# Second block's attention: the older group's value sums follow the third chunk of a unit's transposes and no longer the second

## The reference

```python
def scores(qn_, qr_, kn_, kr_):
    s = jnp.einsum('bqhd,bkhd->bhqk', qn_, kn_) + jnp.einsum('bqhr,bkr->bhqk', qr_, kr_)
    return s.astype(jnp.float32) * scale

def attend(blk):
    qn_b, qr_b = blk
    s = jnp.concatenate([scores(qn_b, qr_b, kn, kr), scores(qn_b, qr_b, knc, krc)], axis=-1)
    p = jax.nn.softmax(s, axis=-1).astype(v.dtype)
    return (jnp.einsum('bhqk,bkhd->bqhd', p[..., :L], v)
            + jnp.einsum('bhqk,bkhd->bqhd', p[..., L:], vc))
```

## Time and profile before

| | us |
|---|---|
| median of 3 runs | 3123.01 (3120.47 to 3127.02) |
| the profiled execution | 3127.2 |
| its span | 3125.4 |
| TensorE busy in the span | 2817.5 (90%) |
| VectorE, ScalarE, GpSimd busy | 1834.8, 883.5, 668.6 |
| mean granted TensorE clock | 0.954 of 2.4 GHz |

### The profile page before, as it was taken

The page is one execution under the profiler, slowest core; times in us unless marked ns, Lnnn a source line. Parts: engine busy times, 40 slices in busy tenths (PEclk is TensorE's granted clock), DMA queues, the critical chain, the costliest instruction groups (busy, mean ns, idle before and its releaser), DMA issues. The chain is left out here.

```text
span 3125.4 us, 30778 instructions
## 1 busy us (share of the span) xinstructions
PE 2817.5 (90%) x11545; PEld 1900.7 (61%) x11545; DVE 1834.8 (59%) x2979; ACT 883.5 (28%) x1527; POOL 668.6 (21%) x408
## 2 busy tenths in 40 slices
PE   5999888988679979999998799996999998999968
PEld 1444444547545548667777699995778885444456
DVE  5644009999576657765841355553685533887553
ACT  1111013100323332245333555552332221111122
POOL 0000000004021112333421333323332220333222
PEclk9999999999879989999999899998999998999979
DMA  2113100000100023333745233223421113111042
GB/s 74 71 72 131 44 20 28 34 34 22 54 1 1 1 91 112 116 127 137 268 168 178 78 88 78 55 58 115 142 88 48 46 69 145 57 57 57 27 168 101
DMA packets 103896, 254.91 MB, mean 82 GB/s; under 512 B 17728, under 2 KB 33768, under 8 KB 99465
## 3 DMA queue, kind: packets, MB, share of 16 engines
q1 hardware_dynamic: 103754, 253.02, 24.3%
HBM read 195.20 MB, written 57.78 MB: 81 GB/s over the span
## 5 line engine op out<-in xcount | busy, mean ns | idle before, releaser
L310 PE MATMUL psum<-part,part 128*128 128x512 f32 (+1 forms) x1984 | 776.7, 391 | 74.9 <-DVE part L2564 25.5
L311 PE MATMUL psum<-part,part 128*128 128x512 f32 (+1 forms) x1984 | 739.3, 373 | 0.0
L312 PE MATMUL psum<-part,part 128*128 128x512 f32 (+1 forms) x1984 | 738.7, 372 | 0.0
L1529 POOL TENSOR_TENSOR part<-arena,part 128x1024 fp32r<-128x1024 f32 (+2 forms) x155 | 353.3, 2280 | 872.5 <-ACT part L1523 872.3
L310 PEld LDWEIGHTS psum<-part,part 128*128 128x128 f32 x1984 | 376.9, 190 | 161.9 <-POOL part L1529 58.1
L311 PEld LDWEIGHTS psum<-part,part 128*128 128x128 f32 x1984 | 377.5, 190 | 78.4 <-issue 12.2
L312 PEld LDWEIGHTS psum<-part,part 128*128 128x128 f32 x1984 | 376.4, 190 | 71.0
L218 PE MATMUL psum<-arena 128*128 128x512 f32 (+1 forms) x672 | 231.8, 505 | 14.7 <-DMA arena<-in_w_f 10.0
L1523 ACT ACTIVATE part<-arena 128x1024 fp32r<-128x1024 f32 (+2 forms) x155 | 149.6, 965 | 271.1 <-PE psum L312 202.4
L2270 DVE TENSOR_REDUCE arena<-psum 128x1 f32<-128x1280 f32 x64 | 95.4, 1491 | 206.4 <-PE psum L2221 206.4
L627 PE MATMUL psum<-arena 128*128 128x512 f32 x464 | 202.1, 597 | 5.7 <-DVEq L417 5.7
(11 more groups left out here) (306 smaller groups left out, 4025.3 us busy)
## 6 DMA issues: line engine op xcount, KB each, us to landing
arena<-in_ada_w SPq DMA_DIRECT2D x24, 1024.0 KB, 6.1
arena<-in_w_hy SPq DMA_DIRECT2D x40, 512.0 KB, 3.2
scratch_spec<-arena SPq DMA_DIRECT2D x68, 256.0 KB, 2.0
arena<-scratch_spec SPq DMA_DIRECT2D x12, 1024.0 KB, 5.3
arena<-in_w_out SPq DMA_DIRECT2D x16, 512.0 KB, 3.6
arena<-in_w_mgate SPq DMA_DIRECT2D x16, 512.0 KB, 4.2
arena<-in_w_mout SPq DMA_DIRECT2D x16, 512.0 KB, 3.7
arena<-in_w_hout SPq DMA_DIRECT2D x16, 512.0 KB, 3.5
```

Of the source, the lines that this page charges most:

```text
L310: nc.tensor.matmul(acc, a_hi, b_hi, start=start, stop=False)
L311: nc.tensor.matmul(acc, a_hi, b_lo, start=False, stop=False)
L312: return nc.tensor.matmul(acc, a_lo, b_hi, start=False, stop=stop)
L1529: self.K.nc.gpsimd.tensor_tensor(self.lo[s][:, 0:n], self.raw[s][:, 0:n], self.hi[s][:, 0:n].bitcast(F32), ALU.subtract).then_inc(self.spl ...
```

## The change

In TensorE's loop the call for the third chunk is put ahead of the values, so that all ten transposes of a unit stand together and the values follow them. The condition on u is tested a second time as a block of its own. Nothing else is changed: no wait, no buffer, no other engine's list.

```diff
@@ -2255,10 +2255,10 @@
                     pe.wait_ge(exped, u + 1)
                     turn(u, 0)
                     turn(u, 1)
+                if 0 <= u < NU:
+                    turn(u, 2)
                 if i >= 3 and (i - 3) // 2 < NU // 2:
                     add_values((i - 3) // 2, (i - 3) % 2)
-                if 0 <= u < NU:
-                    turn(u, 2)
```

## The result

The changed kernel's median is 3230.9 us (4 runs, 3225.66 to 3237.81) against 3123.0 before: a ratio of 1.0346, 95% interval 1.0321 to 1.037. The forecast was 3230.6. The profiled execution of the changed kernel has a span of 3236.0 us, 110.6 more than before.

The account below looks back on a forecast made before the run. TensorE was taken to bound the changed stage; 107.4 us for 60 intervals and 0.2 for the last stretch, added to 3123.0, gave 3230.6 us. Forecast's own range 3224 to 3236; 8-in-10 range 3219 to 3248.

Parts of the forecast that it names:

- The bound: In the changed stage TensorE is busy 362.37 of 367 us, so whatever is added to its path comes out at the end.
- the sum: Over the changed stage: 107.4 us for 60 iteration intervals plus 0.2 at the end, +107.6 us.
- the clock rival: TensorE's clock falls in the new gaps before chunk 2, slower still: 3248 us (one in six) to 3333; chance 0.10.
- The wait: Chunk 2's transposes wait for VectorE's subtraction of chunk 0; TensorE idles about 1.5 us; an iteration without values lasts 5.78 us.
- The values: Fifteen value matmuls on TensorE, put after the wait, are paid in full: 1.80 us an iteration.
- The last stretch: From the transposes of iteration 63 to the reciprocal: 7.82 us against 7.65, +0.2 us.
- The other side: Reordering frees chunk 2 earlier for VectorE, so no slower or faster: 3088 to 3123 us; chance 0.02.
- Part paid back: The wait before chunk 2 shortens in the steady state, loss below 102 us, 3213 us; chance 0.04.
- What was queued behind: Values, next scores and ScalarE's copy of the sums come after the wait; cost nothing, 12 us if the cover failed.

Follow-up runs that it names:

- The dose of values: Changed kernel with two or four of the five key blocks of values put back ahead of chunk 2: 3185.7 and 3143.3 us.
- the neighbouring order: Changed kernel with the two 512-key spans of the next unit's scores put between chunk 1 and chunk 2, values still last: 3156.9 us.
- the run with the copy: Kernel before with a 128x384 SBUF copy added on VectorE ahead of each unit's three subtractions: 3149.5 us.
- both kernels with chunk 0 first: Kernel before with VectorE's subtraction of chunk 0 ahead of the reduction: 3134.9 us alone, 3143.0 us with the added VectorE copy.

## Why the prediction was right

*The bound.* TensorE was the bound of the stage, and idle time put on it came out at the end in full: 108.5 us between iterations 3 and 63, for 107.4 in the sum. That the medians agree to 0.3 us is luck: the interval of the ratio is some 15 us wide, and 1.5 of the 108.5 us come from one iteration that the sum did not have (under the clock rival).

*The wait.* Taken from iterations 1 and 2 of before, where the new order ran already; it was met to a hundredth (2.61 us to chunk 2, 1.57 idle, iteration 7.57 for a forecast of 7.58). The dose of values lies on a straight line, and the iteration of 5.78 us with scores in the gap and the values last shows that it is this wait and no property of the values' place. The gap alone would have given 60 x 1.57 = 94 us. The sum had to be made from whole iterations: the listed idle time starts only behind the recorded tail of the eighth transpose (eight are recorded with 1.03 us, while before the values started 0.79 us after them), so it leaves out 0.24 us of each wait.

*The values.* 1.80 us taken, 1.88 measured as the distance from their first start to the next scores; the first score matmul after them is quicker by what the first value matmul is slower, so that 7.57 comes out.

*The last stretch.* +0.2 forecast, +0.3 measured (7.92 for 7.65).

*The clock rival.* It decided nothing, but was there once. The stretches of the changed kernel around it, and the timelines of TensorE and VectorE:

```profile
1775.00:1779.00 4.00, 2.08 (x17) 1.84 (x16) 2.84 (x4) 2.28 (x3) 1.60 (x1) 0.94 0.01 2
1779.00:1783.00 4.00, 4.00 (x21) 3.83 (x21) 0.43 (x1) 1.46 (x4) 2.41 (x1) 0.64 0.00 0
...
1778.42 0.67 PE L2230 MATMUL psum<-arena 128*128 128x128 f32 x2 [1.92 <-DVE part L2283]
...
1777.61 0.15 DVE L2274 TENSOR_SCALAR arena<-arena 128x1 f32<-128x1 f32 x1 [0.46 <-DVE arena L2270]
```

In iteration 5 the scaling on VectorE started late, 0.46 us after the reduction where it otherwise follows in 0.11, the gap was 1.92 us instead of 1.57, and the clock fell after it: (0.06 + 0.36) x 4 / 0.5 = 3.4 us at the lower level, 1.7 us lost. That iteration took 9.42 us. The same late scaling stands in iteration 5 of the kernel before (at 1772.57, where the iteration took 6.15 us for 5.79), so it is not the change's; its cause stays open. The 61 gaps of 1.57 us, that of 1.50 and that of 0.98 had no fall behind them. The edge was thus nearer than the two gaps of before could tell. The sentence of the Trainium skill on TensorE pausing between groups ("TensorE: Matmul & The Clock Gate", section "A second HAM failure mode: psum-queue depth-cycling") describes what happened once here and did not in the other 63 iterations.

*The other side.* Nothing was freed for anybody: VectorE's wait for chunk 2 is 0.56 us in both kernels. *Part paid back:* none, as the distance to chunk 2 stayed at 2.6 us in all doses.

*What was queued behind.* The cost of nothing for ScalarE's copy held for this change. The slack did not hold in the neighbouring order, by 22.5 us of waits.

## What to carry to other kernels

An instruction that waits for a buffer should have work in front of it as long as the chain that frees the buffer, and a trace can show the uncovered form already, in the first iterations of a pipelined loop where one of its parts isn't there yet: compare whole iterations with and without the part, not gaps. On the engine that is the bound, the order is right when each of its waits ends just before it arrives; a reordering that relieves one should be checked against all the others, also those that come once in eight iterations. That the engine one waits for is idle for 40% of the time says nothing on how much delay it can take at that place.

## What the runs showed of the hardware

The clock's fall went by small differences. After idle stretches of 1.57 us, 61 times, the granted clock stayed at 1.00, while one of 1.92 us in the same loop had some 3.4 us of the lower level behind it. So had all seven of some 3.2 us at the head boundaries, and the one of 2.06 us in the run with the copy (0.60 over the 4 us from 1908), where gaps of up to 1.84 us had none. The length alone does not decide it. In both kernels with chunk 0 first, with and without the copy, the eight transposes of iteration 64 wait 2.08 us for the exponential. First the kernel without the copy, then the one with it:

```profile
2118.32 1.39 PE L2230 MATMUL psum<-arena 128*128 128x128 f32 x8 [2.08 <-ACT arena L2330]
...
2118.00:2122.00 4.00, 3.33 (x25) 2.85 (x25) 1.81 (x3) 1.98 (x6) 0.00 (x0) 1.00 0.00 0
...
2123.49 1.97 PE L2230 MATMUL psum<-arena 128*128 128x128 f32 x8 [2.08 <-ACT arena L2331]
...
2122.00:2126.00 4.00, 2.51 (x12) 2.50 (x13) 2.00 (x5) 2.79 (x5) 0.00 (x0) 0.68 0.00 0
```

The first stayed at 1.00, also in the next 4 us; the second fell, with 0.89 in the next 4 us: (0.32 + 0.11) x 4 / 0.5 = 3.4 us at the lower level. What parts them is not shown. An idle stretch of about 2 us on TensorE cost 1.7 us beyond its length in some of these cases and nothing beyond it in others.

A copy from SBUF to SBUF on VectorE, 128x384 in 0.35 us, took up to 2.36 us beside a multiplication on GpSimd that took 2.37, while the subtractions out of PSUM kept their 0.68 us throughout. By the Trainium skill, page "SBUF — State Buffer", section "SBUF: two separate sides", VectorE and GpSimd share a pair of ports that is held for a whole instruction by the one that came first, where VectorE's instruction is of a kind that needs it; the trace agrees with that for the copy, whose 14 drawn-out cases all began beside a GpSimd instruction and ended 0.2 us after it.
